# Fewer breaks in a stream of weight products, and a throwaway product behind each break (one core, two transformer blocks at 256 tokens)

## The reference, cut to what matters

```python
def hybrid_mixer(h, w_in, b_f, conv_w, out_gain, w_out):
    z = h @ w_in                        # q, k, v | gate_b, gate_c, hc | forget logits
    ...
    attn = forgetting_attention(q, k, v, log_f)            # 8 heads of 128
    conv = gate_b * short_conv(gate_c * hc, conv_w)        # width 3, 1024 channels
    y = jnp.concatenate([attn, conv], axis=-1).reshape(Bsz, L, N_GROUPS, GROUP_DIM)
    y = rmsnorm(y, out_gain.reshape(N_GROUPS, GROUP_DIM)).reshape(Bsz, L, D_MIX)
    return y @ w_out
```

## Time and profile before

| | |
|---|---|
| device time, 3 runs | 2320.62 us median (2319.84 to 2320.70) |
| profiled execution | 2319.24 us, its span 2317.5 us |
| TensorE matmul busy | 2306.0 us, 100% of the span, granted clock 1.00 |
| weight loads busy | 2256.9 us (97%) |
| VectorE, ScalarE busy | 1660.5 us (72%), 1124.2 us (49%) |

### The profile page before, as it was taken

One profiled execution on the slowest core, in us unless ns is written; L12 is line 12 of the kernel. 1 busy time (PEld: TensorE's weight loads), 2 busy tenths in 40 slices (PEclk: granted clock), 3 DMA queues, 4 the chain that ended last, 5 costly groups with the idle time before them and its releaser, 6 DMA issues.

```text
span 2317.5 us, 49716 instructions
## 1 busy us (share of the span) xinstructions
PE 2306.0 (100%) x19252; PEld 2256.9 (97%) x19252; DVE 1660.5 (72%) x2503; ACT 1124.2 (49%) x1503; POOL 0.2 (0%) x4
## 2 busy tenths in 40 slices
PE   9999999999999999999999999999999999999998
PEld 9999999999999999999989988799999999999998
DVE  6687778788878888788887755567666566655665
ACT  6455545544445553445523342455554355544554
POOL 0000000000000000000000000000000000000000
PEclk9999999999999999999999999999999999999999
DMA  7876667588778887887667622065666666655664
GB/s 283 295 286 206 214 222 258 186 304 302 271 253 288 300 282 243 275 285 261 201 227 274 239 74 91 24 208 166 195 195 195 193 191 194 192 197 191 192 195 142
DMA packets 141889, 509.19 MB, mean 220 GB/s; under 512 B 15824, under 2 KB 17360, under 8 KB 141392
## 3 DMA queue, kind: packets, MB, share of 16 engines
q1 hardware_dynamic: 141776, 507.60, 65.6%
HBM read 505.44 MB, written 2.10 MB: 219 GB/s over the span
## 4 chain that ended last, share of the span: by engine, by line
PE 98%; DVE 1%; ACT 0%; DMA 0%; SPq 0%; issue 0%; ACTq 0%
PE ps L1211 30%; PE ps L1212 30%; PE ps L1213 30%; PE ps L1238 1%; PE ps L1239 1%; PE ps L1240 1%; PE ps L1589 1%; PE ps L1702 1%; PE ps L1329 0%; PE ps L1394 0%; PE ps L1580 0%; PE ps L1696 0%; PE ps L1419 0%; PE ps L1635 0%; PE ps L1571 0%; PE ps L1377 0%
## 5 line engine op out<-in xcount | busy, mean ns | idle before, releaser
L613 ACT ACTIVATE hi<-raw 128x1024 fp32r<-128x1024 f32 x654 | 693.0, 1062 | 806.2 <-PE ps L1213 728.5
L1791 DVE TENSOR_TENSOR lo<-raw,hi 128x1024 fp32r<-128x1024 f32 x652 | 794.5, 1221 | 388.0 <-ACT hi L613 384.2
L1211 PE MATMUL ps<-hs,hi 128*128 128x256 f32 (+1 forms) x3040 | 851.6, 280 | 0.4 <-DVE hs L2621 0.3
L1212 PE MATMUL ps<-hs,hi 128*128 128x256 f32 (+1 forms) x3040 | 850.9, 280 | 0.0
L1213 PE MATMUL ps<-hs,lo 128*128 128x256 f32 (+1 forms) x3040 | 850.9, 280 | 0.0
L1211 PEld LDWEIGHTS ps<-hs,hi 128*128 128x128 f32 x3040 | 570.6, 188 | 5.5 <-DVE hs L2621 0.8
L1212 PEld LDWEIGHTS ps<-hs,hi 128*128 128x128 f32 x3040 | 570.9, 188 | 4.5
L1213 PEld LDWEIGHTS ps<-hs,lo 128*128 128x128 f32 x3040 | 570.6, 188 | 4.4
L1211 PE MATMUL ps<-hid,hi 128*128 128x256 f32 x1408 | 388.6, 276 | 0.0
L1213 PE MATMUL ps<-hid,lo 128*128 128x256 f32 x1408 | 388.6, 276 | 0.0
L1212 PE MATMUL ps<-hid,hi 128*128 128x256 f32 x1408 | 388.6, 276 | 0.0
(11 more groups left out here) (350 smaller groups left out, 2725.7 us busy)
## 6 DMA issues: line engine op xcount, KB each, us to landing
raw<-in_stream SPq DMA_DIRECT2D x753, 512.0 KB, 4.3
wm<-in_mod_stream SPq DMA_DIRECT2D x192, 512.0 KB, 4.8
out_tokens<-y_final SPq DMA_DIRECT2D x4, 512.0 KB, 3.7
h<-in_tokens SPq DMA_DIRECT2D x3, 544.0 KB, 8.9
cx<-in_ctx_tokens SPq DMA_DIRECT2D x6, 256.0 KB, 6.0
cbx<-in_c_rows SPq DMA_DIRECT2D x1, 1024.0 KB, 7.6
cbc<-in_c_rows SPq DMA_DIRECT2D x1, 1024.0 KB, 8.0
na<-in_na_bias SPq DMA_DIRECT2D x1, 1024.0 KB, 5.0
```

The source lines that it names most:

```text
L613: act.activation(ring(hi_a, hi, v, slot), raw[:, slot, :], ACT.Copy).then_inc(hi_done, 1)
L1211: pe.matmul(acc_, w_hi[:, w], x_hi, start=kt == 0, stop=False)
L1212: pe.matmul(acc_, w_hi[:, w], x_lo, start=False, stop=False)
L1791: dve.tensor_tensor(ring(lo_a, lo, v, slot), raw[:, slot, :], ring(hi_a, hi, v, slot).bitcast(F32), ALU.subtract)\
```

## The change

Four edits:

1. In `conv1`, `mix` of a head moves from behind chunk 2 to the start of the next half, and `head_stats` from behind the next half's chunk 0 to its start (the head's number is one lower there, so that its squares are long ready). With `scores` they form one break at the start of a half; `transposed` stays behind chunk 1 as the only other break. `conv_stats` of halves 4 and 7 goes to the start of halves 5 and 8.
2. `scores` issues both query-key products first, then both forget terms.
3. Behind each of these breaks stands a product of 128 x 512, `first_opener`: into bank 6 at the start of halves 0 to 8, into bank 5 behind `transposed` of halves 0 to 7; 17 in all.
4. In `q1` the value transposes come two groups at a time, behind chunks 0, 4 and 8.

ScalarE's `take_y` moves along with `mix`, to ahead of `exps` of the next half.

```diff
@@ ScalarE, conv1
                 if hf >= 1:
                     prepare(conv, 0, hf - 1, 3)
+                if 1 <= hf <= HEADS:
+                    take_y(hf - 1)
                 if hf < HEADS:
                     exps(hf)
...
                 prepare(conv, 0, hf, 2, 3)
-                if hf < HEADS:
-                    take_y(hf)
@@ TensorE
+            def opener(bank, x):
+                pe.matmul(ps[:, bank, :].rearrange("p (a n) -> p a n", a=2), x[:, 0, 0:P], x, start=True, stop=True)
+
+            def first_opener(bank):
+                opener(bank, xs1[:, :, 0, NM:N1])
@@ q1
-                    if n % 2 == 0 and n < 12:
+                    if n % 4 == 0 and n < 12:
                         values_by_token(n // 2)
+                        values_by_token(n // 2 + 1)
@@ scores
-                    s = ps[:, 4 + qt, 0:N1]
-                    pe.matmul(s, z[:, 16 + hd, q0:q0 + P], z[:, hd, :], start=True, stop=False)
-                    pe.matmul(s, row, flr[:, 0, :], start=False, stop=True).then_inc(s_ready, 1)
+                    q0 = NM + qt * P
+                    pe.matmul(ps[:, 4 + qt, 0:N1], z[:, 16 + hd, q0:q0 + P], z[:, hd, :], start=True, stop=False)
+                for qt in range(2):
+                    pe.matmul(ps[:, 4 + qt, 0:N1], row, flr[:, 0, :], start=False, stop=True).then_inc(s_ready, 1)
@@ conv1
             for hf in range(LY["conv1"].halves):
+                if 1 <= hf <= HEADS:
+                    mix(hf - 1)
+                if 2 <= hf <= HEADS:
+                    head_stats(hf - 2)
+                if hf in (5, 8):
+                    conv_stats(2 * (hf // 3) - 2)
                 if hf < HEADS:
                     scores(hf)
+                if hf <= HEADS:
+                    first_opener(6)
                 conv_piece(hf, 0)
-                if 1 <= hf <= HEADS:
-                    head_stats(hf - 1)
-                if hf in (4, 7, 10):
-                    conv_stats(2 * (hf // 3) - 2)
+                if hf == HEADS:
+                    head_stats(HEADS - 1)
+                if hf == 10:
+                    conv_stats(4)
...
                 if hf < HEADS:
                     transposed(hf)
+                    first_opener(5)
                 conv_piece(hf, 2)
-                if hf < HEADS:
-                    mix(hf)
                 conv_piece(hf, 3)
```

More of the change, by code:

```diff
@@ L1370, in scores @@
                 for qt in range(2):
-                    q0 = NM + qt * P
                     if hd == 0:
@@ L1460, in pair_of @@
                 return lambda kt: (x[:, kt, 0, :], x[:, kt, 1, :])
-            def opener(bank, x):
-                pe.matmul(ps[:, bank, :].rearrange("p (a n) -> p a n", a=2), x[:, 0, 0:P], x, start=True, stop=True)
             def out_piece(hf, j, turn):
```

## The result

The changed kernel takes 2324.52 us (median of 17 runs, 2323.15 to 2326.56), the kernel before 2320.39 us (17 runs, 2319.17 to 2322.16). The ratio is 1.0018, 95% interval 1.0012 to 1.0025: 4.1 us slower, 2.8 to 5.8 by the interval. The forecast was 2320.3, with a range of 2319.2 to 2324.6; it had the sign wrong, and the time is the one that it gave to its first rival, 2324.3. It lies inside the range only because the range took that rival in.

What follows compares the result with a forecast made beforehand. TensorE (PE) was taken to bound the kernel, busy 100% of the span. The terms 0 - 0.1 + 3.7 - 4.0 + 0.1 = -0.3 us gave 2320.3 against 2320.62 us, range 2319.2 to 2324.6.

Steps and rivals of the forecast that it cites:

- first rival: conv1's pace at 258 columns does not move and the products only cost 3.7 us: 2324.3 us; chance 0.22.
- The faster pace: In conv1, 744 products behind the 512-column ones run faster: -4.0 us taken, from 0 to -4.9.
- the wait in half 0: The first transposes wait 0.74 us for the probabilities, so the added product at half 0's start is free.
- the sign of being wrong: In the changed profile, 119.9 ns a product behind the added 512-column products, where 114 to 116 would be right.
- The rule it rested on: Behind each of the eight 512-column products, the next 256-column products run at the faster pace from the start, 4.5 ns apart.
- The price of the products: Each 512-column product costs about 0.23 us to the next start; 16 x 0.233 = +3.7 us, the one in half 0 free.
- Merging breaks is free: Moving mix, head_stats and conv_stats in conv1: a merged break costs its parts and no more, 0 us.
- Scores in pairs: Both query-key products before both forget terms in scores: 0 us taken, bounds -0.15 to 0 over eight heads.
- q1: Six breaks become three; of six fast chunks three may be lost: +0.1 us taken, cases +0.3, 0 and -0.6.
- The wait ahead of the transposes: In conv1, a new wait if the probabilities' chain slips over 1.7 us; 2327.6 us at 1 us over; chance 0.07.
- The rule from the Trainium skill: Gap of N/2.4 + 2.5 ns without memory: 216 ns per 512-column product, no gain, 16 of them +3.5 us.
- Faster by over 0.2%: A gain of 4.6 us, needing the pace gain of all 744 products and the openers for nothing; chance 0.03.

Runs made afterwards that it cites:

- out1_no_product: The kernel before without its one 512-column product in out1 at 360.67 us; 2333.88 us, ratio 1.0058.
- no_products: The changed kernel without its 17 products of 128x512, merged breaks, paired scores and q1's pairs kept; 2320.10 us, ratio 0.9998 to the kernel before.
- q1_pairs_only: The kernel before with only q1's value transposes taken two groups at a time, three breaks for six; 2321.18 us, ratio 1.0001.
- plain_ring: The changed kernel with `SHIFTED = 0`, so that all weight copies lie in rows of 1024 floats, not 1040; 2325.53 us in one execution.

## Why the prediction was wrong, point by point

**The step that failed** is the one that gave the faster pace to conv1: "The faster pace: it would cover 96 products in halves 1 to 7 ... I take -4.0". It measured 0.0: 119.6 to 120.3 ns by chunk behind the products, as before (the one chunk with the wait in half 0 apart), and the prediction had named 119.9 ns as the sign of being wrong. So of the sum the cost stayed and the gain did not. The forecast took two paces seen at 256 aligned columns, a product that stood at the turn, and carried both to 258 columns from column 14. It named the reason against (never fast in 48 chunks, columns that start at 14) and gave it 0.22. Cutting the columns to 256 at the same start left 120.0 ns, and an aligned start with 258 gave 121.5, so neither half of the difference was harmless.

**The rule it rested on was itself too simple.** "Behind each of the eight 512-column products the next 256-column products run at the faster one from the start" was true of that trace, and in out1 such a product is the cause (117.8 to 113.35 ns, and 256 columns don't do it). But in conv1 at 256 aligned columns it brings no fast chunk more, and at 435.96 of out1_no_product the pace stays at 117.8 ns. Nor does one of the eight places hold by itself: behind the 512-column product at 1152.65 us the next 144 products run at 113.3 ns in both profiles of the kernel before and in the changed one, and at 117.8 in ten of the 17 kept profiles, no_products and q1_pairs_only among them. Eight agreeing places in one trace were read as a law of the operation.

**The price of the products** was right: 0.23 us each, and the sum of 3.7 for 16 of them. The seventeenth was to be hidden by the wait in half 0. It is: 7.84 us from scores to transposes with it, 7.83 without. In the changed kernel's own profile the wait is 0.9 us and this distance 8.26, which belongs to its late start.

**Merging breaks is free** was right: 15.07 against 15.09 us a half. Scores in pairs, 0: nothing to be seen either.

**q1** was right in size: +0.1 taken, 0.18 measured, with four fast chunks left where three or six were the two cases.

**The wait ahead of the transposes** (a rival with 0.07) didn't come: in halves 1 to 7 no wait of PE is in the profile, the 1.7 us to spare held. Moving take_y, mix and VectorE's later reading of the banks stayed hidden.

**The rule from the Trainium skill**, "TensorE: Matmul & The Clock Gate", section "Back-to-back issue gap": as a price without memory it gave +3.5 us, and for this change it was nearer than the sum. The section calls its formula the gap of an isolated product and says that in a stream with weight loads 512 columns take less, about 131 ns; the prediction left that out, and the traces, with 233 ns, don't show it. For out1 the formula is not enough, since there a single product is worth 13.6 us.

**Faster by over 0.2%** needed what no row gave; it didn't happen.

## What to carry to other kernels

A product that nobody reads is a cost that is certain and a pace that is not: before placing 17 of them, place one and read the distance between starts behind it, in the layer itself with its own width and start column. Where a stream of weight products is the bound, read its pace per chunk, since the busy share is 100% at either pace: here 256 columns from column 16 reach 114 ns in some chunks of conv1, the same from column 14 run at 120.0, and 4.5 ns a product over 3000 products is 13.5 us. And an observation that holds at every place of one trace is still one experiment: a second profile of the same kernel, or the product taken away at one place, would have shown that it isn't the rule.

## What the runs showed of the hardware that was not expected

One 512-column product, 0.23 us from its start to the next, is worth 13.6 us: without it 600 products behind it run at 117.8 instead of 113.35 ns, and so do the 2232 behind the next breaks, although a product of the same kind stands ahead of them. The granted clock is 1.00 over both stretches, in either kernel. Something carries over breaks of narrow products and into the next layer that the pace alone doesn't show: the 24 products between run at 117.8 ns in both kernels. A product of 256 columns doesn't set it, one of 512 sets it in some places and not in others.

The pattern of fast and slow chunks agrees in both profiles of the kernel before at every place but one, though waits and arrivals differ between them. So most of it follows from the order of the instructions and their addresses. The exception is the run at 1587 us, whose six chunks differ between two executions of one program: there the moment decides too, and it comes behind a wait of 0.3 us for VectorE. The two profiled spans, 2317.5 and 2318.1 us, differ by about its 0.7 us.

What the state is stays open: the ring's place changes the pattern (plain_ring), a product changes it, the width and the start column change it, and no run here separates the weight reads from the column reads. It also stays open what the faster pace would be worth to conv1 if its token rows were laid out so that its columns started aligned: 258 columns from column 0 were slower, and the kernel with 256 columns from 16 and no products was 3.5 us faster than before, in one execution, with two columns of work left out.
